# Attention's sums with the values standing still and the turned probabilities moving, and the softmax division moved to ScalarE

## The chip, the cores and the metric

The kernel runs on one core of a Trainium2 chip. Its engines are PE (TensorE, matrix multiply), DVE (VectorE), ACT (ScalarE), POOL (GpSimd) and SP (SyncE, which issues the weight loads). Each follows its own list of instructions in order, and they meet only by semaphores. The metric is the device time of one execution in microseconds (us), the median of several runs.

## The reference

A causal decoder trunk of two layers over 256 tokens of width 1024. Every layer is half a SwiGLU block, a mixer, and another half SwiGLU block, each behind an RMSNorm and added to x. The first layer's mixer has two groups of heads side by side: eight heads of softmax attention (MLA) and eight heads of a gated delta rule. Their results stand side by side (512 columns each) and go through one output projection:

```python
def one_block(args):                     # MLA attention, one block of 128 queries
    q_blk, blk = args
    sc = jnp.einsum('bhqd,bhkd->bhqk', q_blk, kh) * scale
    q_idx = blk * ATTN_BLOCK + jnp.arange(ATTN_BLOCK)
    sc = jnp.where(key_idx[None, :] <= q_idx[:, None], sc, -jnp.inf)
    p = jax.nn.softmax(sc, axis=-1)
    return jnp.einsum('bhqk,bhkd->bhqd', p, vh)
...
y = jnp.concatenate([y_mla, o.reshape(b, s, GDN_HEADS * GDN_DV)], axis=-1)
return y @ w_out
```

The softmax weights of a query are exp(score) over their sum; they then weigh the values v, 64 features per head. The delta rule needs decay matrices, triangular systems of 64x64 per head and chunk, and a scan over four chunks. Everything is float32.

## The kernel before

Matrix products of weights are made of three products of parts rounded to PE's fast float type ("hi" and "lo"): ScalarE writes the hi part of each weight unit (function hi), VectorE or POOL the lo part, and the same is done with the activations.

The change lies in the first layer's mixer, between 268 and 300 us of the execution. There the kernel runs the eight attention heads one after another, and lays the preparation of the delta rule between them. The 256 tokens are two tiles of 128, so a head has three blocks of 128x128 scores: queries 0 with keys 0, queries 1 with keys 1, queries 1 with keys 0. Per head h:

- PE makes the scores (head_scores, L1912) in one of two banks.
- VectorE finds each row's maximum (row_max, L1325 to L1327) and sends it on as the bias of the exp.
- ScalarE writes exp of the three blocks to probs (exps, L753 and L755) and gets the sum of each row beside it (row_sum). probs has two slots.
- PE turns the three blocks (transposes, L2012), ScalarE copies the result to pT (L771), and PE multiplies (weighted_values, L1927): the turned probabilities are loaded as weights, 128 columns each, and v moves, 64 columns each. The result has the tokens on the partitions and lies in banks 0 and 1.

The rows are divided by their sums at the very end: when all heads are done, VectorE takes one reciprocal of all 16 sums per token (L1405) and multiplies both banks by it on the way to Y (L1408, "y_mla"). PE then turns Y (y_transposes, L2050), ScalarE rounds it to hTh (yT_hi, L803), and VectorE writes the rest to hTl (yT_lo, L1415).

Each engine's order is written out by hand in its own block, with waits on semaphores. PE starts with head_scores of heads 0 and 1; then for each h come transposes(h), head_scores(h+2), weighted_values(h-1) and pieces of the delta rule (decay_rows, head_transposes, gram, problems). ScalarE's list has for each h the copy to pT, pieces of the delta rule (after head 0 two copies of Z, L776, and small exps, L784 to L786; after heads 1 to 4 dT_out, L761; after head 2 the exp of Dec, L791) and exps(h+2). VectorE's has row_max(h+2) and, between, norms of the delta rule's heads (L1349), the decay differences (L1377), products (L1385, L1392) and D (L1397, L1398).

Behind the heads VectorE makes ten masked blocks (L1366), the division, the first pair of N1 (L1428), two products with the decay (L1437) and yT_lo. PE takes the first two m1 products (L1981), y_transposes, and then a loop of small products for the triangular systems; its second step in that loop, dt_next(0, 1), writes to banks 0 and 1 and so waits for yT_lo. Behind that comes early (L2061), the first part of the output projection, which needs the lo parts of weights that POOL makes (L459) once the masked blocks are done. ScalarE writes two units' hi parts (L500) before yT_hi.

```python
pe.wait_ge(S("exp_done"), 2 * h + 2)                # before transposes(h)
dve.wait_ge(S("score_sums"), h + 1)                 # before row_max(h)
if n == 0:
    pe.wait_ge(S("yT_lo"), 4)                       # before dt_next(0, 1)
sp_.wait_ge(S("v_sums"), 4)                         # before the loads of the next SwiGLU's weights
```

## Time and profile before

| | |
|---|---|
| median of 3 runs | 1062.76 us (1062.66 to 1063.14) |
| the profiled execution | 1061.91 us, of which the span of the profile is 1060.0 |
| PE busy | 1046.9 us (99%), 8325 matmuls |
| VectorE (DVE) busy | 809.8 us (76%) |
| ScalarE (ACT) busy | 562.6 us (53%) |
| POOL busy | 46.7 us (4%) |
| chain that ended last | PE 80%, DVE 14%, issue 3%, ACT 2% |

The shares are means over the whole span; what the change meets is read from the stretch of the heads. The profile has six views that matter here: the page with totals; busy time by stretch; the chain of waits, which goes back from the last instruction to what released each step; the timeline of one engine, with the idle time ahead of an instruction and what ended it; one line of the program with its durations; and groups by line and shape.

### The profile page before, as it was taken

To read this page: it belongs to the slowest core of one execution; us is meant where nothing else is said; L and a number is where in the kernel's file an instruction comes from. 1 tells how busy PE (TensorE), PEld (TensorE's weight loads), DVE (VectorE), ACT (ScalarE), POOL (GpSimd) and SP (SyncE) were. 2 spreads that over 40 slices of the span, in tenths; PEclk is the share of its full clock that TensorE was granted. 3 is DMA by queue.
4 is the path that set the end of the run, shared out by engine and by line. 5 is a ranking of instruction groups with operands and counts; after the bars stand their busy time and mean duration, and the time that the engine had idled before them with its cause. 6 is when DMAs were issued, how large, how long until landed. Compare 5 with 4: busy or idle time off the path is not lost.

```text
span 1060.0 us, 19231 instructions
## 1 busy us (share of the span) xinstructions
PE 1046.9 (99%) x8325; PEld 960.7 (91%) x8325; DVE 809.8 (76%) x1072; ACT 562.6 (53%) x695; POOL 46.7 (4%) x32
## 2 busy tenths in 40 slices
PE   9999999999999999999999999999999999999998
PEld 8999987998878999998799999878888889999986
DVE  5887789899854776778987677898666548676797
ACT  6654545685873644445554444555664436444451
POOL 1000000110190000000000000001000000000000
PEclk9999999999999999999999999999999999999999
DMA  9756566463003555565556556566654546555551
GB/s 308 250 187 190 171 199 198 154 202 116 2 5 108 180 192 184 176 198 198 198 163 195 177 182 197 198 201 226 187 164 162 192 155 205 172 187 190 171 196 41
DMA packets 127214, 184.91 MB, mean 174 GB/s; under 512 B 4221, under 2 KB 101738, under 8 KB 127002
## 3 DMA queue, kind: packets, MB, share of 16 engines
q1 hardware_dynamic: 126384, 181.85, 53.1%
q0 software_dynamic: 448, 1.71, 0.5%
q8 instruction: 66, 1.08, 0.4%
q10 hardware_dynamic: 298, 0.12, 0.1%
q14 instruction: 18, 0.15, 0.0%
HBM read 182.62 MB, written 1.05 MB: 173 GB/s over the span
## 4 chain that ended last, share of the span: by engine, by line
PE 80%; DVE 14%; issue 3%; ACT 2%; DMA 1%; SPq 0%; ACTq 0%; DVEq 0%
PE banks L1528 22%; PE banks L1530 22%; PE banks L1529 22%; DVE wlo L968 3%; DVE arena L1040 2%; DVE rounded L1048 2%; PE banks L1689 1%; PE banks L1690 1%; PE banks L1691 1%; DVE arena L1041 1%; DVE raw L1042 1%; PE banks L1981 1%; DVE wlo L1050 1%; PE banks L1606 1%; PE banks L1607 1%
## 5 line engine op out<-in xcount | busy, mean ns | idle before, releaser
L960 DVE TENSOR_TENSOR wlo<-raw,whi 128x2048 fp32r<-128x2048 f32 (+2 forms) x141 | 318.7, 2271 | 101.7 <-ACT whi L500 101.7
L500 ACT ACTIVATE whi<-raw 128x2048 fp32r<-128x2048 f32 (+3 forms) x169 | 309.1, 1841 | 155.9 <-PE banks L1530 138.5
L1528 PE MATMUL banks<-xTh,whi 128*128 128x256 f32 x1360 | 385.3, 283 | 0.2 <-DVE wlo L960 0.2
L1530 PE MATMUL banks<-xTh,wlo 128*128 128x256 f32 x1360 | 384.9, 283 | 0.0
L1529 PE MATMUL banks<-xTl,whi 128*128 128x256 f32 x1360 | 384.9, 283 | 0.0
L1528 PEld LDWEIGHTS banks<-xTh,whi 128*128 128x128 f32 x1360 | 261.1, 192 | 0.4 <-DVE wlo L960 0.4
L1529 PEld LDWEIGHTS banks<-xTl,whi 128*128 128x128 f32 x1360 | 261.1, 192 | 0.0
L1530 PEld LDWEIGHTS banks<-xTh,wlo 128*128 128x128 f32 x1360 | 261.1, 192 | 0.0
L1528 PE MATMUL banks<-whi,hTh 128*128 128x512 f32 (+1 forms) x192 | 77.8, 405 | 1.6 <-DVE wlo L1050 1.6
L1530 PE MATMUL banks<-whi,hTl 128*128 128x512 f32 (+1 forms) x192 | 74.7, 389 | 0.0
L1529 PE MATMUL banks<-wlo,hTh 128*128 128x512 f32 (+1 forms) x192 | 74.5, 388 | 0.0
L562 ACT ACTIVATE rounded<-arena 128x1536 fp32r<-128x1536 f32 x24 | 35.8, 1492 | 67.4 <-DVE raw L1042 67.4
L1528 PE MATMUL banks<-whi,xTh 128*128 128x512 f32 (+1 forms) x160 | 63.2, 395 | 0.0
L556 ACT ACTIVATE rounded<-arena 128x512 fp32r<-128x512 f32 x24 | 15.2, 632 | 88.6 <-DVE arena L1024 88.6
L1530 PE MATMUL banks<-whi,xTl 128*128 128x512 f32 (+1 forms) x160 | 61.9, 387 | 0.0
L1529 PE MATMUL banks<-wlo,xTh 128*128 128x512 f32 (+1 forms) x160 | 61.8, 386 | 0.0
L1606 PE MATMUL banks<-whi,hTh 128*128 128x512 f32 x144 | 56.2, 391 | 0.0
L1607 PE MATMUL banks<-wlo,hTh 128*128 128x512 f32 x144 | 56.1, 390 | 0.0
L1528 PEld LDWEIGHTS banks<-whi,hTh 128*128 128x128 f32 x192 | 36.1, 188 | 12.2 <-DVE wlo L1050 5.0
L1610 PE MATMUL banks<-whi,hTl 128*128 128x512 f32 x144 | 44.4, 389 | 0.0
L1008 DVE TENSOR_TENSOR arena<-banks,arena 128x512 f32<-128x512 f32 x44 | 30.4, 691 | 17.9 <-PE banks L1530 17.2
L1530 PEld LDWEIGHTS banks<-whi,hTl 128*128 128x128 f32 x192 | 36.0, 188 | 7.7
(298 smaller groups left out, 1566.0 us busy)
## 6 DMA issues: line engine op xcount, KB each, us to landing
raw<-in_ffn_w_down SPq DMA_DIRECT2D x44, 1024.0 KB, 4.9
raw<-in_ffn_w_gate SPq DMA_DIRECT2D x43, 1024.0 KB, 5.3
raw<-in_ffn_w_up SPq DMA_DIRECT2D x43, 1024.0 KB, 5.4
raw<-in_sg_w_in SPq DMA_DIRECT2D x16, 1024.0 KB, 5.5
raw<-in_ab_w_in SPq DMA_DIRECT2D x8, 1024.0 KB, 5.1
raw<-in_sg_w_out SPq DMA_DIRECT2D x8, 1024.0 KB, 4.8
raw<-in_ab_w_out SPq DMA_DIRECT2D x4, 1024.0 KB, 4.9
raw<-in_ab_w_in SPq DMA_DIRECT2D x2, 832.0 KB, 4.4
```

The source lines that it names most:

```text
L500: A(whi[:, j % SLOTS, 0:n], raw[:, j % RAW_SLOTS, 0:n], ACT.Copy).then_inc(S("hi_ready"), 1)
L562: A(T_HI[k % 2], T_SUM[k % 2], ACT.Copy).then_inc(S("sums_hi"), 1)
L960: TT(wlo[:, j % RAW_SLOTS, 0:n], raw[:, j % RAW_SLOTS, 0:n], whi[:, j % SLOTS, 0:n].bitcast(f32), ALU.subtract).then_inc(S("lo_ready"), 1)
L968: TT(wlo[:, j % RAW_SLOTS, 0:1536], raw[:, j % RAW_SLOTS, 0:1536], whi[:, j % SLOTS, 0:1536].bitcast(f32), ALU.subtract)
L1008: TT(prod[:, c % 2, :], B[PAIR_BANK[c][1]][:], gate[:, c % 2, :], ALU.mult).then_inc(S("prod_ready"), 1)
L1040: link(TT(t3[:, 0:2, :], b[:, 1:3, :], bc(b[:, 3:4, :], [P, 2, 512]), ALU.add))
L1528: mm(out_ap, lh, rh, start=first, stop=False)
L1529: mm(out_ap, lh, rl, start=False, stop=False)
L1530: return mm(out_ap, ll, rh, start=False, stop=last)
L1606: mm(o, hTh[:, kk, tok], wh[:, k, c], start=kk == 0, stop=False)
L1607: mm(o, hTh[:, kk, tok], wl[:, k, c], start=False, stop=False)
L1610: last = mm(o, hTl[:, kk, tok], wh[:, k, c], start=False, stop=False)
```

## The change

The probabilities are divided by their sums before they are turned, and the second product is made the other way round.

- VectorE has a new step sum_inverse(h): it waits for both exps of head h and takes the reciprocal of its 128x2 sums. The steps for heads 0 and 1 stand ahead of the rsqrt chain, the others between the pieces for the delta rule, that for head 7 behind the first masked block. The reciprocal of all sums and the two y_mla multiplications behind the heads are gone. head_sums(1), a row sum for the delta rule, moves from behind row_max(1) to ahead of the small copies that come before row_max(0).
- ScalarE has a new step scale_probs(h): it waits for sum_inverse(h) and multiplies the head's probabilities by it in place, 128x128 and 128x256. scale_probs(0) stands behind exps(1), scale_probs(h+1) behind the copy to pT of head h.
- PE's transposes(h) wait for scale_probs(h) and no longer for the exp. In weighted_values v is now loaded as weights (64 columns) and the turned probabilities move: one product with 256 columns (both blocks of keys 0) and one with 128. The result has features on the partitions, as the output projection wants it, so Y and y_transposes(0, 4) are gone for this half; yT_hi waits for the last weighted_values.
- Two semaphores of POOL become one (dec_then_vb), with the same order.

In ScalarE's list around heads 0 to 2 there stood before (L753 and L755 are exps of heads 0, 1 and then 2, L680 a copy for the convolution, L771 the copy to pT, L776 the copies of Z):

```order
L753 ACTIVATE arena,small<-banks,small 128x128 [waits softmax_in]
L755 ACTIVATE arena,small<-banks,small 128x256
L753 ACTIVATE arena,small<-banks,small 128x128 [waits softmax_in]
L755 ACTIVATE arena,small<-banks,small 128x256
L680 ACTIVATE arena<-banks 128x2x256 [waits nt_sums]
L771 ACTIVATE arena<-banks 128x384 [waits pT_sums]
L776 ACTIVATE arena<-banks,small 128x512 [waits head_sums,unit_done]
L776 ACTIVATE arena<-banks,small 128x512
L784 ACTIVATE small<-banks 64x2x4 [waits gc_ready]
L784 ACTIVATE small<-banks 64x2x4 x3
L785 ACTIVATE small<-small 128x16
L786 ACTIVATE small<-small 128x16
```

Nothing stands there between the exps of head 1 and the copy to pT but one copy. Now the same stretch reads (L768 and L769 are scale_probs of heads 0 and 1, L779 the copy to pT, L786 the copies of Z):

```order
L753 ACTIVATE arena,small<-banks,small 128x128 [waits softmax_in]
L755 ACTIVATE arena,small<-banks,small 128x256
L753 ACTIVATE arena,small<-banks,small 128x128 [waits softmax_in]
L755 ACTIVATE arena,small<-banks,small 128x256
L768 ACTIVATE arena<-arena,small 128x128 [waits sum_inverted]
L769 ACTIVATE arena<-arena,small 128x256
L680 ACTIVATE arena<-banks 128x2x256 [waits nt_sums]
L779 ACTIVATE arena<-banks 128x384 [waits pT_sums]
L768 ACTIVATE arena<-arena,small 128x128 [waits sum_inverted]
L769 ACTIVATE arena<-arena,small 128x256
L786 ACTIVATE arena<-banks,small 128x512 [waits head_sums,unit_done]
L786 ACTIVATE arena<-banks,small 128x512
```

Two pairs of scaled copies have come in, the first ahead of the first copy to pT, the second ahead of the copies of Z, and both wait for VectorE's reciprocals.

In VectorE's list from row_max(7) to yT_lo there stood before (L1366 the masked blocks, L1405 the reciprocal, L1408 y_mla, L1428 N1, L1437 the products with the decay, L1415 yT_lo; the first row is the bias of head 7):

```order
L1327 SCALAR_TENSOR_TENSOR small<-small 128x1
L1366 TENSOR_TENSOR arena<-banks,C 128x512 [waits seed_sums] x4
L1366 TENSOR_TENSOR arena<-banks,C 128x512 [waits score_sums,seed_sums]
L1366 TENSOR_TENSOR arena<-banks,C 128x512 [waits seed_sums] x4
L1366 TENSOR_TENSOR arena<-banks,C 128x512 [waits score_sums,seed_sums]
L1405 RECIPROCAL small<-small 128x16 [waits exp_done]
L1408 TENSOR_TENSOR arena<-banks,small 128x512 [waits pv_sums,dve_chain]
L1408 TENSOR_TENSOR arena<-banks,small 128x512
L1428 TENSOR_TENSOR arena<-C,banks 128x512 [waits m1_sums] x2
L1437 TENSOR_TENSOR arena<-banks,arena 128x8x64 [waits gram_sums,dec_masked]
L1437 TENSOR_TENSOR arena<-banks,arena 128x8x64 [waits gram_sums]
L1415 TENSOR_TENSOR hTl<-banks,hTh 128x256 [waits yT_hi] x4
```

The blocks followed each other without a wait for an exp, and the division stood behind them. Now the same stretch reads (L1343 sum_inverse(7), L1383 the masked blocks, L1446 N1, L1455 the products, L1433 yT_lo):

```order
L1337 SCALAR_TENSOR_TENSOR small<-small 128x1
L1383 TENSOR_TENSOR arena<-banks,C 128x512 [waits seed_sums]
L1343 RECIPROCAL small<-small 128x2 [waits exp_done]
L1383 TENSOR_TENSOR arena<-banks,C 128x512 [waits seed_sums] x3
L1383 TENSOR_TENSOR arena<-banks,C 128x512 [waits score_sums,seed_sums]
L1383 TENSOR_TENSOR arena<-banks,C 128x512 [waits seed_sums] x4
L1383 TENSOR_TENSOR arena<-banks,C 128x512 [waits score_sums,seed_sums]
L1446 TENSOR_TENSOR arena<-C,banks 128x512 [waits m1_sums] x2
L1455 TENSOR_TENSOR arena<-banks,arena 128x8x64 [waits gram_sums,dec_then_vb]
L1455 TENSOR_TENSOR arena<-banks,arena 128x8x64 [waits gram_sums]
L1433 TENSOR_TENSOR hTl<-banks,hTh 128x256 [waits yT_hi] x4
```

Three instructions are gone between the masked blocks and N1, and a reciprocal that waits for the last exp has come in behind the first masked block.

The diff:

```diff
--- before.py
+++ after.py
@@ -452,8 +452,8 @@
             pool.wait_ge(S("decb_ready"), 1)
             pool.wait_ge(S("softmax_in"), HEADS)
             D3 = Dec.rearrange("p (m j) -> p m j", j=64)
-            mul(D3, D3, bc(const("causal").unsqueeze(1), [P, NT * HEADS, 64])).then_inc(S("dec_masked"), 1)
-            per_head(QKVn[2].rearrange("p t n -> p (t n)"), QKVn[2], beta).then_inc(S("vb_ready"), 1)
+            mul(D3, D3, bc(const("causal").unsqueeze(1), [P, NT * HEADS, 64])).then_inc(S("dec_then_vb"), 1)
+            per_head(QKVn[2].rearrange("p t n -> p (t n)"), QKVn[2], beta).then_inc(S("dec_then_vb"), 1)
             def pool_lo(j):
                 pool.wait_ge(S("hi_ready"), j + 1)
                 nc.gpsimd.tensor_tensor(wlo[:, j % RAW_SLOTS, :], raw[:, j % RAW_SLOTS, :],
@@ -761,14 +761,24 @@
                 A((kT, qT)[i // 2][:, 2 * (i % 2):2 * (i % 2) + 2, :],
                   B[3][:].rearrange("p (q n) -> p q n", n=SEQ), ACT.Copy).then_inc(S("dT_out"), 1)
 
+            def scale_probs(h):
+
+                act.wait_ge(S("sum_inverted"), h + 1)
+                p = probs[h % 2]
+                A(p[:, 0, :], p[:, 0, :], ACT.Copy, scale=rden[:, 0, h:h + 1])
+                A(p[:, 1:3, :], p[:, 1:3, :], ACT.Copy, scale=rden[:, 1, h:h + 1]).then_inc(S("probs_scaled"), 1)
+
             exps(0)
             exps(1)
+            scale_probs(0)
             nt_out(5)
             for h in range(HEADS):
                 act.wait_ge(S("pT_sums"), h + 1)
                 if h >= 2:
                     act.wait_ge(S("pv_sums"), h - 1)
                 A(pT[:, h % 2, :], B[4][:, 0:3 * P], ACT.Copy).then_inc(S("pT_out"), 1)
+                if h + 1 < HEADS:
+                    scale_probs(h + 1)
                 if h == 0:
                     act.wait_ge(S("unit_done"), Z_UNIT + 2)
                     act.wait_ge(S("head_sums"), 2)
@@ -799,7 +809,7 @@
 
             def yT_hi(k0, k1):
                 for k in range(k0, k1):
-                    act.wait_ge(S("yT_sums"), k // 2 + 1)
+                    act.wait_ge(*((S("pv_sums"), HEADS) if k < 4 else (S("yT_sums"), k // 2 - 1)))
                     A(hTh[:, k, :], B[YT_BANK[k // 2]][:, 256 * (k % 2):256 * (k % 2) + 256], ACT.Copy
                       ).then_inc(S("yT_hi"), 1)
 
@@ -1327,6 +1337,12 @@
                 STT(nbias[:, h % 2, 1:2], m[:, 1:2], m[:, 2:3], q_nscale[:, 1, h:h + 1], ALU.max, ALU.mult
                     ).then_inc(S("softmax_in"), 1)
 
+            def sum_inverse(h):
+
+                dve.wait_ge(S("exp_done"), 2 * h + 2)
+                nc.vector.reciprocal(rden[:, :, h], row_sum[:, :, h]).then_inc(S("sum_inverted"), 1)
+
+            head_sums(1)
             gcf, ekf = (a.rearrange("p t h -> p (t h)") for a in (gc, ek))
             dve.wait_ge(S("gc_sums"), 2)
             for c in range(2):
@@ -1339,7 +1355,8 @@
             dve.wait_ge(S("q_scaled"), 2)
             row_max(0)
             row_max(1)
-            head_sums(1)
+            sum_inverse(0)
+            sum_inverse(1)
             dve.wait_ge(S("head_sums"), 2)
             both = qk_head_ss.rearrange("p a m -> p (a m)")
             link(rsqrt(both, both, 2 * M, 1.0))
@@ -1370,15 +1387,19 @@
             for h in range(HEADS):
                 if 0 < h < HEADS - 2:
                     row_max(h + 2)
+                if h == 0:
+                    sum_inverse(h + 2)
                 if h == 1:
                     dve.wait_ge(S("gc_ready"), 1)
                     for t in range(NT):
                         dve.wait_ge(S("gr_sums"), t + 1)
                         link(TT(h3(Dec, t), B[(5, 2)[t]][:].rearrange("p (h j) -> p h j", j=64),
                                 bc(gcf[:, 8 * t:8 * t + 8].unsqueeze(2), [P, HEADS, 64]), ALU.subtract))
+                    sum_inverse(3)
                     TS(Dec, Dec, 0.0, None, ALU.max).then_inc(S("dec_diff"), 1)
                 if h == 2:
                     head_norm(QKVn[0], 0, float(DK) ** -0.5).then_inc(S("heads_normed"), 1)
+                    sum_inverse(4)
                     dve.wait_ge(S("decay_exps"), 2)
                     link(TT(begc, beta, egc, ALU.mult))
                     dve.wait_ge(S("decay_exps"), 3)
@@ -1391,23 +1412,20 @@
                         dst, decay = decay_products(odd, Lm, DecB)
                         TT(dst, B[(5, 2)[odd]][:].rearrange("p (q j) -> p q j", j=64), decay, ALU.mult
                            ).then_inc(S("decayed"), 1)
+                    sum_inverse(5)
                 if h == 4:
                     dve.wait_ge(S("decayed"), 2)
                     for t in range(NT):
                         link(TT(h3(D, t), h3(Lm, t), eight("first"), ALU.mult))
                         TT(h3(D, t), eight("eye64"), h3(D, t), ALU.subtract).then_inc(S("d_ready"), 1)
-
-            for n in range(5):
+                    sum_inverse(6)
+
+            masked_block(0, 0)
+            sum_inverse(7)
+            for n in range(1, 5):
                 masked_block(0, n)
             for n in range(5):
                 masked_block(1, n)
-            dve.wait_ge(S("exp_done"), 2 * HEADS)
-            link(nc.vector.reciprocal(rden, row_sum))
-            dve.wait_ge(S("pv_sums"), HEADS)
-            for t in range(NT):
-                TT(Y[:, t, 0:512].rearrange("p (h d) -> p h d", d=VDIM),
-                   B[t][:].rearrange("p (h d) -> p h d", d=VDIM),
-                   bc(rden[:, t, :].unsqueeze(2), [P, HEADS, VDIM]), ALU.mult).then_inc(S("y_mla"), 1)
 
             def yT_lo(k0, k1):
                 for k in range(k0, k1):
@@ -1430,7 +1448,7 @@
                        two_banks((M1_BANKS if n else M1_FIRST)[t]).rearrange("p o (m j) -> p o m j", j=64), ALU.subtract
                        ).then_inc(S("m1_ready"), 1)
                 if n == 0:
-                    dve.wait_ge(S("dec_masked"), 1)
+                    dve.wait_ge(S("dec_then_vb"), 1)
                     for odd in range(2):
                         dve.wait_ge(S("gram_sums"), odd + 3)
                         dst, decay = decay_products(odd, Am, Dec)
@@ -1922,10 +1940,12 @@
                 pe.wait_ge(S("pT_out"), h + 1)
                 if h == 0:
                     pe.wait_ge(S("z_out"), 2)
-                e = slice(VDIM * h, VDIM * h + VDIM)
-                for t, i, tk, a, z in ((0, 0, 0, True, True), (1, 1, 1, True, False), (1, 2, 0, False, True)):
-                    last = mm(B[t][:, e], pT[:, h % 2, P * i:P * i + P], kv_v[:, tk, h, :], start=a, stop=z)
-                last.then_inc(S("pv_sums"), 1)
+                o = B[h // 4][HC[h % 2], 256 * (h // 2 % 2):256 * (h // 2 % 2) + 256]
+                blocks3 = pT[:, h % 2, :].rearrange("p (b n) -> p b n", n=P)
+                mm(o.rearrange("p (b n) -> p b n", n=P), kv_v[:, 0, h, :], blocks3[:, 0:3:2, :], start=True, stop=False,
+                   skip_group_check=True)
+                mm(o[:, P:2 * P], kv_v[:, 1, h, :], blocks3[:, 1, :], start=False, stop=True, skip_group_check=True
+                   ).then_inc(S("pv_sums"), 1)
 
             eye = const("eye64")
 
@@ -2005,7 +2025,7 @@
             head_scores(1)
             to_tokens(5)
             for h in range(HEADS):
-                pe.wait_ge(S("exp_done"), 2 * h + 2)
+                pe.wait_ge(S("probs_scaled"), h + 1)
                 if h:
                     pe.wait_ge(S("pT_out"), h)
                 for i in range(3):
@@ -2071,8 +2091,6 @@
             m1(0, 0)
             pe.wait_ge(S("lt_level"), 10)
             m1(0, 1)
-            pe.wait_ge(S("y_mla"), 2)
-            y_transposes(0, 4)
             for n in range(4):
                 pe.wait_ge(S("m1_ready"), 2 * n + 1)
                 if n:
@@ -2128,7 +2146,7 @@
                 last.then_inc(S("qdT_sums"), 1)
             pe.wait_ge(S("at_ready"), 2)
 
-            pe.wait_ge(S("vb_ready"), 1)
+            pe.wait_ge(S("dec_then_vb"), 2)
 
             def heads(): return [(q, odd, 2 * q + odd) for q in range(PAIRS) for odd in range(2)]
 
```

## Rows read from the trace of the kernel before

**Rows 1.** The page's first line
```profile
span 1060.0 us, 19231 instructions
```

**Rows 2.** Busy time by stretch: PE, PEld, DVE, ACT, POOL, then PEclk, DMA share, GB/s
```profile
268.00:276.00 8.00, 7.03 (x51) 4.80 (x50) 7.42 (x28) 6.95 (x26) 0.00 (x0) 1.00 0.00 0
276.00:284.00 8.00, 8.00 (x127) 7.54 (x125) 7.80 (x18) 6.81 (x19) 0.00 (x0) 1.00 0.01 2
284.00:292.00 8.00, 7.62 (x167) 7.06 (x165) 7.01 (x14) 4.59 (x14) 3.32 (x2) 1.00 0.01 3
292.00:300.00 8.00, 6.54 (x279) 5.78 (x281) 7.93 (x17) 7.04 (x11) 6.29 (x3) 1.00 0.02 5
```

**Rows 3.** The chain of waits in order of time: start us, us, what
```profile
288.32 0.21 DVE small L1327
...
289.06 3.77 DVE arena L1366 x7
...
295.92 1.27 DVE arena L1428 x2
...
298.33 1.40 DVE hTl L1415 x4
...
299.86 0.41 PE banks L1981 x11
...
300.96 0.43 PE banks L1528
```

**Rows 4.** Timeline of PE: start us, us, what [idle before <-releaser]
```profile
269.65 0.55 PE L2012 MATMUL banks<-C,arena 128*128 128x128 f32 x3 [0.84 <-ACT arena L755]
...
277.00 0.78 PE L1927 MATMUL banks<-arena 128*128 128x64 f32 x6
...
294.57 0.69 PE L1981 MATMUL banks<-arena 64*64 64x64 f32 x32 [0.21 <-DVE arena L1366]
```

**Rows 5.** Timeline of ScalarE (ACT), the same columns
```profile
270.38 0.20 ACT L755 ACTIVATION_READ_ACCUMULATOR arena<-banks,small 128x1 f32 x1
...
270.47 0.60 ACT L680 ACTIVATE arena<-banks 128x512 f32<-128x512 f32 x1
...
270.94 0.50 ACT L771 ACTIVATE arena<-banks 128x384 f32<-128x384 f32 x1
...
271.31 1.29 ACT L776 ACTIVATE arena<-banks,small 128x512 f32<-128x512 f32 x2
...
274.13 0.46 ACT L753 ACTIVATE arena<-banks,small 128x128 f32<-128x128 f32 x1 [0.57 <-DVE small L1327]
...
275.03 0.20 ACT L755 ACTIVATION_READ_ACCUMULATOR arena<-banks,small 128x1 f32 x1
...
292.56 3.71 ACT L500 ACTIVATE whi<-raw 128x2048 fp32r<-128x2048 f32 x2
```

**Rows 6.** Timeline of VectorE (DVE), the same columns
```profile
270.45 0.18 DVE L937 TENSOR_SCALAR small<-small 128x32 f32<-128x32 f32 x1
...
275.15 0.55 DVE L1325 TENSOR_REDUCE small<-banks 128x3 f32<-128x384 f32 x1
...
278.78 1.22 DVE L1349 SCALAR_TENSOR_TENSOR arena<-arena,small 128x1024 f32<-128x1024 f32 x1
...
287.66 0.56 DVE L1325 TENSOR_REDUCE small<-banks 128x3 f32<-128x384 f32 x1 [0.88 <-PE banks L1912]
...
294.44 0.24 DVE L1405 RECIPROCAL small<-small 128x16 f32<-128x16 f32 x1
```

**Rows 7.** Line 671 alone: durations ns min/median/max, first and last start
```profile
L671 ACT ACTIVATE arena<-arena,param_cols x12: 493/496/510, 214.9 to 251.7; 128x256 f32<-128x256 f32 x12
```

**Rows 8.** Groups by line and form, 262 to 300: busy us, mean ns
```profile
L1927 PE MATMUL banks<-arena 128*128 128x64 f32 x48 | 6.3, 268 | 0.0
...
L1935 PE MATMUL banks<-arena,C 64*64 64x512 f32 x8 | 2.2, 611 | 0.1
```

**Rows 9.** Timeline of POOL (GpSimd)
```profile
294.62 9.07 POOL L459 TENSOR_TENSOR wlo<-raw,whi 128x2048 fp32r<-128x2048 f32 x2 [1.71 <-DVE arena L1366]
```

## The prediction

> **What bounds the kernel now.** I read the page's first line, then the busy time by stretch, then the chain of waits, then each engine's timeline around the attention heads. The profiled execution took 1061.91 us, 1060.0 of it the span [rows 1], 0.85 less than the median 1062.76 of the three runs; the change below is worked out inside that span and then added to the median. It acts between 268 and 300 us. There [rows 2] the granted clock is 1.00, and of each 8 us PE is busy 7.03, 8.00, 7.62 and 6.54, VectorE 7.42, 7.80, 7.01 and 7.93, ScalarE 6.95, 6.81, 4.59 and 7.04. So PE and VectorE run neck and neck through the heads, ScalarE has 5.7 us free in the first three stretches, and after 292 VectorE leads. The chain [rows 3] agrees: behind the heads it runs through VectorE's masked blocks, the first pair of N1 at 295.92, the products with the decay and the four yT_lo from 298.33, and comes back to PE at 299.86, at the first step that needs yT_lo. From there PE leads. The weight loads of the next part wait for v_sums, which lies behind this, so nothing keeps its old time and a shift at 299.86 goes through to the end.
>
> **What goes.** From the start of the reciprocal, 294.44, to that of N1, 295.92 [rows 3, 6], VectorE's path loses 1.48 us: the reciprocal and both y_mla. PE's eight transposes of y_mla go too; I count them at nothing, since PE waits for VectorE's decay products and yT_lo right behind them. The yT_hi on ScalarE lose their wait for PE, but stand behind two weight copies (hi), 292.56 to 296.27 [rows 5].
>
> **What comes on ScalarE and VectorE.** A scaled copy of 128x256 within SBUF takes 0.50 us [rows 7]. ScalarE's slope is 0.9 ns per column (1.85 for one of 2048 columns against 0.37 from 270.94 to 271.31 for 384 [rows 5]), so one of 128x128 takes 0.39. An instruction lets the next start 0.13 before its own end (270.94 plus 0.50 against 271.31). So scale_probs holds ScalarE for 0.65 us per head and its result stands 0.77 after its start; eight make 5.2 us. A reciprocal of 128x16 takes 0.24 [rows 6]; one of 128x2 isn't in the trace. Between nothing and 0.24 I take 0.1 of queue.
>
> **What comes on PE.** The old sums are six instructions of 64 moving columns: 0.78 us, less the last one's own 0.27, is 0.51 from first to last start, 0.10 each [rows 4, 8]. The new ones are two passes of 256 columns and two of 128. 448 more columns cost 0.61 - 0.27 = 0.34 [rows 8], so 768 columns take 0.59 where the six took 0.61. If the four loads of 64 columns came on top, at half of 0.10, it would be 0.2 more per head. Bounds: nothing and 0.2; I take 0.1, most of which falls into PE's new waits.
> The Trainium skill ("TensorE: Matmul & The Clock Gate", Part 3, The mechanism) says that a weight load overlaps running matmuls only where the row group differs. All loads here use all 128 rows, so by it the 0.2 would be due and the sum below would be 2.0 instead of 1.8. The trace can't decide: 0.10 fits a covered load as well as half of one followed by 64 columns.
>
> **What comes on the path.** Now transposes(h) wait for scale_probs(h), that for sum_inverse(h) on VectorE, and that for the last exp of h. Behind a waiting inverse stand the next row_max and all of VectorE's decay work.
> *Heads 0 and 1.* head_sums(1) moves ahead into idle time, but the inverse of head 1 waits for the second exp, whose sum is out at 270.58 [rows 5]. With the wake-up and both reciprocals the rsqrt chain starts near 270.8, not 270.45 [rows 6]: 0.35 later.
> *Head 2.* ScalarE takes its next instruction at 270.47, so the first scaled probabilities stand at 271.24 and transposes(0) start near 271.3, not 269.65 [rows 4]. They take 0.55, pT 0.37, scale_probs(1) 0.65; so the two Z copies start at 272.9, not 271.31. The small exps behind them ended at 273.56 (274.13 less the idle 0.57) and end now at 275.15; exp(2), 1.10 long (274.13 to 275.23), has its sums at 276.25 [rows 5]. VectorE, which was free for row_max(3) at 275.15 [rows 6], comes to the inverse at 275.5, waits 0.8, and row_max(3) starts at 276.4: 1.25 later.
> *Head 4.* ScalarE's queue from 276.15: pT 0.37, scale 0.65, dT_out 0.47 (a 512-wide copy, 270.47 to 270.94), exps 1.0, pT 0.37, scale 0.65, to 279.66; dT_out again with about 0.25 of waiting for PE, the exp of Dec (1024 columns, 0.93 by the slope), exps 1.10: sums out at 282.4 [rows 5]. VectorE left head_norm at 279.92 (278.78 plus 1.22 less overlap [rows 6]), now about 281.5, waits 0.9, and goes on at 282.6: 2.7 later. Head 3's own short wait is contained in that.
> *Heads 5 and 6.* Two reciprocals and a little wait: 2.95 later. But before row_max(7) VectorE idled 0.88, until 287.66, for the scores of head 7 [rows 6]. Now it is the late one: 286.78 plus 2.95, so 289.75, 2.1 later. PE's scores come about then too, since its problems wait for VectorE.
> *Head 7.* From row_max(7) to its bias is 0.87 (288.32 plus 0.21), exp(7) follows with 1.10, so its sum is out 2.0 after row_max(7). Its inverse stands behind the first masked block, which lets go 1.40 after (289.06 [rows 3]). It waits 0.66 and takes 0.1: the masked blocks end 2.86 later.
> *Behind them.* 1.48 less. And the second N1 now meets its matmuls: m1(0,1) begins 0.05 after the last block and takes 0.69 [rows 4], so N1 starts 0.26 later than VectorE could; y_mla covered that.
> Sum at 299.86: 2.1 + 0.76 - 1.48 + 0.26 = 1.64, and with 0.15 for PE's sums **1.8 us later**. Two covers hold: the weight copies start 2.9 later, so the first yT_hi pair is out at 299.7, and VectorE wants it at 300.1; POOL's first split ends at 294.62 + 4.55 + 2.9 = 302.05 [rows 9], and PE wants it at 300.96 + 1.8 = 302.75 [rows 3]. Ends of the unknown: reciprocals, copies and wake-ups each 0.1 cheaper give 1.2; each 0.1 dearer, with PE's 0.2, give 3.0.
>
> **The rivals.**
> *ScalarE becomes the bound* (slower). 18.35 us busy of the first 24, plus 5.2, leaves 0.5 [rows 2]; each head passes its ordered queue three times, and yT_hi has only 0.4 of cover. At the dear end it is 3.0 us and somewhat more, 1065.8 to 1066.5; it decides once a pair of scaled copies holds ScalarE over 0.75. Against it: PE and VectorE have work of their own for most of those waits. VectorE did this scaling in some 1.25 us over 1024 columns, ScalarE gets 3072; were all its 5.2 us on the path, it would be 5.2 - 1.48 = 3.7, so 1066.5.
> The Trainium skill ("ScalarE: Activation LUTs", Rules for kernel authors) gives multiplications to VectorE rather than ScalarE; by that rule this rival would be the likeliest, while the rows show free time on ScalarE for most of the copies.
> *The heads take the lag in* (faster). If ScalarE catches up before exp(2) and exp(4), the waits of 0.8 and 0.9 vanish, the idle 0.88 before row_max(7) takes in the rest, and -1.48 + 0.26 are left: 1061.5. It needs ScalarE to have 1.6 us to spare before exp(2), where it had 0.57 [rows 5].
> *TensorE's clock falls* (slower). PE would idle 0.84 + 1.65 = 2.5 us before transposes(0), where 0.84 were [rows 4]; the granted clock was 1.00 throughout [rows 2]. On the lower of the two levels PE's next four us of work take four more, one to two of which lie in its waits: 2 to 3 on top, 1066.6 to 1067.6.
>
> **How the numbers follow.** The forecast, 1062.76 + 1.8 = 1064.6, has 0.55, ScalarE as the bound 0.28, the clock 0.07, the heads that take it in 0.10. A measurement of this kernel can tell about 0.2%, 2.1 us, from no change; the forecast lies just inside it. Of its 0.55 I put 0.46 inside and 0.09 above; of ScalarE's 0.28, 0.05 inside; all of the clock's above; of the faster case 0.02 inside. That gives slower 0.39, within 0.53, faster 0.08. The forecast's own range is 1063.9 to 1065.8 (1.2 to 3.0 added); for 8 in 10 I take 1062.5 to 1066.8.
>
> **What would show it.** Right: transposes(0) near 271.3; VectorE waiting about 0.8, 0.9 and 0.7 before the inverses of heads 2, 4 and 7; row_max(7) 2.1 and the end of the masked blocks 2.9 later; no wait before yT_lo; the first step behind yT_lo 1.8 later, and the same shift from there to the end. Wrong: row_max(7) unmoved, matmuls at twice their duration behind transposes(0), yT_lo waiting for ScalarE, or a shift that changes after 301.

## The result: slower by 0.5%, outside the range, and the profile after

The changed kernel takes 1068.16 us (median of 6 runs, 1067.25 to 1068.99), the kernel before in the same session 1062.80 (1062.66 to 1063.26, 6 runs): a ratio of 1.005, 95% interval [1.0037, 1.0063]. It is 5.36 us slower; the forecast said 1.8.

The profiled execution of the changed kernel has this first line, beside [rows 1]:

```profile
span 1065.4 us, 19204 instructions
```

Its granted clock is the first thing that differs. These are busy times by stretch, the columns those of [rows 2]: first the 8 us of the first row there, then the same time in pieces of 2 us.

```profile
268.00:276.00 8.00, 5.49 (x29) 3.60 (x27) 5.88 (x25) 7.50 (x26) 0.00 (x0) 0.79 0.00 0
...
270.00:272.00 2.00, 0.59 (x4) 0.59 (x5) 1.12 (x8) 1.85 (x7) 0.00 (x0) 0.90 0.00 0
272.00:274.00 2.00, 2.00 (x11) 1.65 (x12) 1.33 (x8) 1.79 (x5) 0.00 (x0) 0.50 0.00 0
274.00:276.00 2.00, 2.00 (x9) 0.70 (x8) 1.95 (x4) 1.87 (x9) 0.00 (x0) 0.74 0.00 0
276.00:278.00 2.00, 2.00 (x14) 1.29 (x13) 1.26 (x5) 1.72 (x7) 0.00 (x0) 1.00 0.00 0
```

It was 1.00 all through before. Now it is 0.50, the lower of its two levels (1.2 GHz), from about 271.6 to about 275. PE's timeline (start us, us, what [idle before <-releaser]) shows what PE did before and behind:

```profile
268.30 0.60 PE L1839 MATMUL banks<-C,arena 128*128 128x128 f32 x4
271.41 0.76 PE L2032 MATMUL banks<-C,arena 128*128 128x128 f32 x3 [2.51 <-ACT arena L769]
...
273.80 1.66 PE L1955 MATMUL banks<-arena,C 64*64 64x512 f32 x4
275.39 0.55 PE L2032 MATMUL banks<-C,arena 128*128 128x128 f32 x3
```

PE stood still for 2.51 us, waiting for the second scaled copy (L769). Then transposes(0) took 0.76 instead of 0.55 [rows 4], and transposes(1) start at 275.39. In the kernel before they stood at 272.22, behind four products of 512 columns that took 1.07 and now take 1.66:

```profile
271.21 1.07 PE L1935 MATMUL banks<-arena,C 64*64 64x512 f32 x4
272.22 0.55 PE L2012 MATMUL banks<-C,arena 128*128 128x128 f32 x3
```

VectorE's timeline has the waits at the inverses of heads 2, 3, 4 and 7 (L1343), the last row_max (L1335), the masked blocks (L1383) and N1 (L1446):

```profile
276.68 0.17 DVE L1343 RECIPROCAL small<-small 128x2 f32<-128x2 f32 x1 [0.70 <-ACT arena L755]
...
280.94 0.17 DVE L1343 RECIPROCAL small<-small 128x2 f32<-128x2 f32 x1 [1.50 <-ACT arena L755]
...
284.42 0.17 DVE L1343 RECIPROCAL small<-small 128x2 f32<-128x2 f32 x1 [0.80 <-ACT arena L755]
...
292.08 0.56 DVE L1335 TENSOR_REDUCE small<-banks 128x3 f32<-128x384 f32 x1 [0.52 <-PE banks L1930]
...
294.12 0.17 DVE L1343 RECIPROCAL small<-small 128x2 f32<-128x2 f32 x1 [0.56 <-ACT arena L755]
294.21 5.45 DVE L1383 TENSOR_TENSOR arena<-banks,C 128x512 f32<-128x512 f32 x9
299.66 1.51 DVE L1446 TENSOR_TENSOR arena<-C,banks 128x512 f32<-128x512 f32 x2
```

The last row_max stood at 287.66 [rows 6] and N1 at 295.92 [rows 3]: 4.4 and 3.7 later. Then the second surprise, on PE, between the first of the eight early products (L1546 here, L1528 before, where the first stood at 300.96 in the chain [rows 3]) and the fifth:

```profile
304.47 0.50 PE L1546 MATMUL banks<-whi,hTh 128*128 128x512 f32 x1
...
306.06 1.63 PE L2001 MATMUL banks<-arena 64*64 64x64 f32 x96 [0.62 <-issue]
...
309.88 1.29 PE L2001 MATMUL banks<-arena 64*64 64x64 f32 x68 [0.69 <-issue]
...
313.52 0.81 PE L2001 MATMUL banks<-arena 64*64 64x64 f32 x41 [0.50 <-issue]
...
317.14 0.45 PE L2001 MATMUL banks<-arena 64*64 64x64 f32 x12 [0.48 <-issue]
```

Four waits "issue", 2.3 us in all, that no engine ends. In the kernel before there were two in the same stretch, 0.75 in all:

```profile
310.58 0.80 PE L1981 MATMUL banks<-arena 64*64 64x64 f32 x36 [0.20 <-issue]
...
314.26 0.34 PE L1981 MATMUL banks<-arena 64*64 64x64 f32 x8 [0.55 <-issue]
```

In the changed kernel they come 3.6 to 3.8 us apart. From one to the next PE runs 126 to 128 recorded matmuls, each with its weight load. The DMA view of the same kernel from 302 to 322 us (GB/s in slices of 0.5 us; then the queue, its packets, MB) shows what comes at that pace:

```profile
GB/s 0 0 0 33 0 0 0 0 0 0 33 0 0 0 0 0 0 0 33 0 0 0 0 0 0 33 0 0 0 0 0 0 33 0 0 0 0 0 0 0
...
q8 instruction: 5, 0.08, 1.7%
```

A packet of instructions arrives at 303.5, 307, 311, 314.5 and 318, 33 GB/s times 0.5 us or 16.5 KB each, and PE goes on 2.5 to 3 us behind each. The Trainium skill ("Perfetto Trace Analysis", The 4-stage abstract model) says that an instruction has 64 bytes; by that, as an estimate, a packet holds about 256, and the 126 to 128 matmuls with as many loads agree.

To compare kernels whose earlier work drifts by some tenths, I count from the start of the last product of the Z unit ahead of the heads (262.62 before, 262.71 after). Shifts against the kernel before, in us:

| kernel | ratio | transposes(0) | row_max(7) | N1 | first early | eighth early |
|---|---|---|---|---|---|---|
| changed | 1.005 | 1.67 | 4.33 | 3.65 | 3.49 | 5.11 |
| e1 fill, same place | 1.0029 | 1.67 | 2.72 | 2.03 | 3.23 | 4.54 |
| e2 fill, other place | 1.0020 | 1.67 | 2.72 | 2.03 | 2.07 | 3.63 |
| e3 no division | 1.0003 | 0 | 0.84 | -0.40 | -0.57 | 0.47 |
| e4 copies alone | 1.0039 | 1.67 | 5.71 | 5.02 | 4.86 | 7.33 |
| e5 inverses alone | 1.001 | 0 | 0.97 | 0.20 | 0.12 | 2.03 |
| e6 copies, clock held | 1.0017 | 1.66 | 2.67 | 1.98 | 1.82 | 2.84 |
| e7 longer gap alone | 1.004 | 2.51 | 3.67 | 3.68 | 3.46 | 3.94 |
| e8 removal alone | 0.9997 | 0 | 0 | -1.48 | -0.85 | 0.47 |
| e9 gap as after | 1.0028 | 1.71 | 2.82 | 2.82 | 2.61 | 3.46 |
| e10 gap, clock held | 1.0008 | 1.71 | 1.25 | 1.25 | 0.85 | 2.87 |
| e11 before, wide | 0.9969 | 0 | 0 | 0 | -0.27 | -2.39 |
| e12 removal, wide | 0.9969 | 0 | 0 | -1.48 | -0.58 | -2.69 |
| e13 before, all wide | 0.996 | 0 | 0 | 0 | -0.43 | -2.57 |
| e14 removal, all wide | 0.995 | 0 | 0 | -1.48 | -1.59 | -3.74 |
| e15 change, all wide | 0.9982 | 1.67 | 2.71 | 2.02 | 1.86 | -0.29 |

The ratio is over all executions, but the shifts of each row are from one profiled execution. That of the kernel before took 1061.91 us, 1.0 to 1.6 less than its medians in the sessions of the experiments (1062.87 to 1063.49). Up to N1 this does not show. The last column, which contains the "issue" waits, can be too large by about that much: e2 has 3.63 there, and its median is 1.6 above that of the kernel before.

### The profile page after: what moved, and what is told of

It reads as the page before. It is cut to its first block, busy times and chain, and to the rows that moved or that the text cites. A ratio compares the mean times of both kernels' runs of the same rounds, so it can differ in the third digit from the quotient of the medians.

```text
span 1065.4 us, 19204 instructions
## 1 busy us (share of the span) xinstructions
PE 1050.0 (99%) x8301; PEld 959.9 (90%) x8301; DVE 809.4 (76%) x1077; ACT 568.2 (53%) x711; POOL 46.8 (4%) x32
## 3 DMA queue, kind: packets, MB, share of 16 engines
q0 software_dynamic: 448, 1.71, 0.5%
## 4 chain that ended last, share of the span: by engine, by line
PE 80%; DVE 14%; issue 3%; ACT 2%; DMA 1%; SPq 0%; ACTq 0%; DVEq 0%
PE banks L1546 22%; PE banks L1548 21%; PE banks L1547 21%; DVE wlo L978 3%; DVE arena L1050 2%; DVE rounded L1058 2%; PE banks L1707 1%; PE banks L2001 1%; PE banks L1709 1%; PE banks L1708 1%; DVE arena L1051 1%; DVE raw L1052 1%; DVE wlo L1060 1%; PE banks L1624 1%; PE banks L1628 1%
## 5 line engine op out<-in xcount | busy, mean ns | idle before, releaser
L1546 PE MATMUL banks<-xTh,whi 128*128 128x256 f32 x1360 | 385.4, 283 | 0.2 <-DVE wlo L970 0.2
L1546 PEld LDWEIGHTS banks<-xTh,whi 128*128 128x128 f32 x1360 | 261.2, 192 | 0.4 <-DVE wlo L970 0.4
L1546 PE MATMUL banks<-whi,hTh 128*128 128x512 f32 (+1 forms) x192 | 77.7, 405 | 1.5 <-DVE wlo L1060 1.3
L1546 PE MATMUL banks<-whi,xTh 128*128 128x512 f32 (+1 forms) x160 | 63.2, 395 | 0.0
L1546 PEld LDWEIGHTS banks<-whi,hTh 128*128 128x128 f32 x192 | 36.1, 188 | 12.1 <-DVE wlo L1060 4.9
```

Of the source, the lines that this page charges most:

```text
L1546: mm(out_ap, lh, rh, start=first, stop=False)
```

## The experiments

Theory: three things add up, the forecast's mechanism (about 2 us), the fall of the clock (about 1.6) and PE's supply of instructions, which takes back what the removal gains (about 1.2). Rivals: the round trip over VectorE costs it all; ScalarE's queue does, whatever the clock.

### The clock

Both fills keep PE at work in the gap and change nothing else of the changed kernel, e1 by the first loop, e2 by the second:

```diff
             to_tokens(5)
+            for _ in range(12):
+                mm(B[4][:, 3 * P:3 * P + 64], ident, ident[:, 0:64], start=True, stop=True)
...
+            for _ in range(36):
+                mm(B[4][:, 3 * P:4 * P], mask16[:, 0:P], mask16[:, P:2 * P], start=True, stop=True)
```

> The changed kernel with twelve float32 products of 64 columns (24 instructions, results unused) on PE between to_tokens(5) and transposes(0), where PE idled 2.51 us. They also bring PE's list behind y_mla's old place back to the instruction count of the kernel before. Theory 1, the clock: the granted clock stays 1.00 from 270 to 276 us, transposes(0) take 0.55 and not 0.76 us, row_max(7) comes about 2.1 us after that of the kernel before and not 4.4, and the time falls by about 2.3 to 1065.9. Theory 2, PE's waits of 0.5 to 0.7 us without a cause in the trace between 305 and 317 us hang on where PE's list of instructions is cut: with the old count they shrink from 2.3 to about 0.75 us and the time falls by another 1.5, to 1064.4. Rival, the queue on ScalarE bounds whatever PE's clock does: 1068 as the changed kernel.

> As before, but the gap is filled with 36 bfloat16 products of 128 columns, so the clock should hold as well while PE's list behind is 12 instructions pairs longer than in the kernel before. Theory 1: clock 1.00, row_max(7) plus 2.1, about 1065.9 if the unexplained waits stay at 2.3. Theory 2: the waits without a cause move to other places; their sum may come out anywhere between 0.7 and 2.3, so 1064.4 to 1065.9. Rival (ScalarE bounds): 1068.

e1 took 1066.17 us, ratio 1.0029 [1.0018, 1.0040], e2 1065.04, ratio 1.0020 [1.0010, 1.0029]. The second theory of e1 fell: with the old count of instructions the "issue" waits from the first to the eighth early product are still 2.1 us, and two more, 1.7 in all, stand ahead of the first. e2 by stretch and on PE's timeline:

```profile
272.00:274.00 2.00, 2.00 (x15) 1.21 (x13) 1.69 (x10) 1.85 (x5) 0.00 (x0) 1.00 0.00 0
...
269.11 2.17 PE L2028 MATMUL banks<-mask 128*128 128x128 bf16 x36
271.79 0.55 PE L2034 MATMUL banks<-C,arena 128*128 128x128 f32 x3 [0.51 <-ACT arena L769]
```

The clock stays at 1.00, the transposes start at the same place (8.70 us behind the Z unit) and take 0.55, and N1 comes 1.62 us earlier than in the changed kernel. The rival "ScalarE, whatever the clock" falls: only 2.03 of the 3.65 at N1 is left.

The gap alone, put into the kernel before by GpSimd (three products in e7, two in e9, and in e10 two with the 36 products of e2):

```diff
+            pool.wait_ge(S("exp_done"), 2)
+            for _ in range(2):
+                after(mul(at(11008, 256), QKVn[2][:, 0, 0:256], QKVn[2][:, 1, 0:256]))
...
                 pe.wait_ge(S("exp_done"), 2 * h + 2)
+                if h == 0:
+                    pe.wait_ge(S("pool_chain"), 10)
```

> The kernel before, but its first transposes wait for three products of 256 columns on GpSimd behind the exps of head 0, so that PE stands idle some 2.5 us there instead of 0.84; nothing else is changed. Theory (the idle time alone makes the granted clock fall): a stretch of some 4 us from the transposes on below 0.8, transposes(0) 0.7 to 0.8 long instead of 0.55, N1 2 to 4 us later, ratio 1.002 to 1.004. Rival (the clock fell for another reason, or the idle time is harmless): clock 1.00, N1 at most 1.2 us later, ratio 1.000 to 1.0012.

> The kernel before with GpSimd's two products (instead of three) ahead of the first transposes: they should start 8.7 to 8.8 us behind the Z unit's last product, as in the changed kernel; nothing else is changed. Theory (this idle time alone makes the granted clock fall): a stretch of about 4 us from 270 on below 0.8, N1 2.4 to 3.4 us later than in the kernel before, ratio 1.002 to 1.004. Rival (only the longer idle time of the run before did): clock 1.00, N1 at most 1.7 later, ratio at most 1.0015.

> As e9_gap_as_after, with 36 small products on PE in the idle time. Theory (the clock is the larger part of what the idle time costs): clock 1.00, N1 0.5 to 1.5 us later than in the kernel before and at least 1 us earlier than in e9_gap_as_after, ratio 1.0002 to 1.0015. Rival (the late start of the transposes is what costs, whatever the clock): N1 within 0.5 of that of e9_gap_as_after, ratio 1.002 to 1.003.

e7: 1067.67 us, ratio 1.0040 [1.0027, 1.0053]; its gap was 3.35 us, longer than meant, hence e9. Its transposes(0) took 0.52 and not the 0.7 to 0.8 expected; the clock fell just behind them. e9: 1066.31, ratio 1.0028 [1.0018, 1.0038]. e10: 1064.01, ratio 1.0008 [0.9999, 1.0017]. e9 on PE's timeline and by stretch:

```profile
271.88 0.52 PE L2017 MATMUL banks<-C,arena 128*128 128x128 f32 x3 [2.55 <-POOL arena L424]
...
272.00:274.00 2.00, 2.00 (x13) 1.61 (x14) 1.69 (x10) 1.57 (x4) 0.00 (x0) 0.69 0.00 0
274.00:276.00 2.00, 2.00 (x7) 0.52 (x4) 1.93 (x5) 1.88 (x11) 0.00 (x0) 0.50 0.00 0
```

Without any part of the change, the same idle time makes the clock fall; with it held (e10, 1.00 from 268 to 300) N1 comes 1.57 earlier, and the median is 2.3 lower. So 1.6 us at N1 is the clock's price, found twice.

The fall does not come in every execution. Where it came, the mean clock of the whole execution is 0.996 to 0.998. It is 1.00 in one of the eight of e9 (1063.43 us, the others 1065.04 to 1067.24) and in one of the six of e4 below (1065.00, the others 1067.02 to 1070.16). It is 0.998 in one of the nine of e2 (1067.59, the others 1064.50 to 1066.46) and in one of the six of e1 (1068.26, the others 1065.05 to 1066.95). These four differ from the median of the others of their kernel by 2.5 to 3.3 us. They were not profiled, so where their clock fell or held is not shown.

### Which part of the change costs the rest

e3 takes out all steps of the division, e5 only ScalarE's, so in both the transposes wait for the exps. The edit of e3:

```diff
-            scale_probs(0)
...
-                if h + 1 < HEADS:
-                    scale_probs(h + 1)
...
-                nc.vector.reciprocal(rden[:, :, h], row_sum[:, :, h]).then_inc(S("sum_inverted"), 1)
...
-                pe.wait_ge(S("probs_scaled"), h + 1)
+                pe.wait_ge(S("exp_done"), 2 * h + 2)
```

e4 takes out the reciprocal and keeps the copies, which multiply by one:

```diff
-                act.wait_ge(S("sum_inverted"), h + 1)
...
-                A(p[:, 0, :], p[:, 0, :], ACT.Copy, scale=rden[:, 0, h:h + 1])
...
+                act.wait_ge(S("exp_done"), 2 * h + 2)
+                A(p[:, 0, :], p[:, 0, :], ACT.Copy, scale=ones128[:, 0:1])
...
```

e6 is e4 with the 36 products of e2.

> The changed kernel without the division: no sum_inverse, no scale_probs, and transposes(h) wait for the exps as before (the probabilities stay unscaled). What is left is the second product the other way round, without y_mla and PE's y_transposes. My sum says 1.48 less on VectorE, 0.26 back at the second N1 and 0 to 0.15 for PE: 1061.6 to 1061.8, with the clock at 1.00 since transposes(0) start near 269.7. Rival, the new product with 768 columns is what costs: 1063 or more.

> The changed kernel without VectorE's inverses: scale_probs multiplies by a constant of one, waits for ScalarE's own exp and for nobody else. Transposes(0) come about as late as in the changed kernel (271.4), so by theory 1 the clock falls here too, and with it most of the loss stays: 1065.5 to 1067. Rival, the round trip over VectorE (its waits of 0.7, 1.5, 0.8 and 0.56 us before the inverses) is the cause: 1062.5 to 1063.5.

> VectorE makes the eight small inverses where the change puts them, but ScalarE scales nothing and the transposes wait for the exps as before, so the division is left out. Theory (the scaled copies and the idle PE ahead of the first transposes cost the time, the inverses hardly any): transposes(0) 7.0 us behind the last product of the Z unit as in the kernel before, granted clock 1.00, first pair of N1 between 0.4 earlier and 0.5 later than before, ratio 0.999 to 1.001. Rival (VectorE standing at its inverses is what costs): N1 1.5 us or more later, ratio 1.0015 to 1.003.

> Scaled copies by one without inverses (the division is left out), and 36 small products on PE ahead of the first transposes, which keep it from standing idle. Theory (most of what the copies alone lost was the granted clock): clock 1.00 through the heads, first pair of N1 1.5 to 2.2 us later than in the kernel before instead of 5.0, ratio 1.001 to 1.0025. Rival (the copies hold ScalarE's queue, whatever the clock): N1 over 3 us later, ratio 1.003 to 1.005.

e3: 1063.53 us, ratio 1.0003 [0.9994, 1.0011]. e4: 1067.93, ratio 1.0039 [1.0026, 1.0052]. e5: 1063.48, ratio 1.001 [0.9999, 1.002]. e6: 1064.93, ratio 1.0017 [1.0009, 1.0026].

e3 missed: its time lies where the rival had it, and not at 1061.6 to 1061.8. Up to the scores of head 7 PE's list differs from that of before in the new products alone, and PE gets to these scores 0.84 later. So row_max(7) is 0.84 later too, and VectorE waits 1.22 us for it instead of 0.88 [rows 6]:

```profile
289.51 0.56 DVE L1332 TENSOR_REDUCE small<-banks 128x3 f32<-128x384 f32 x1 [1.22 <-PE banks L1926]
```

So without any division the new products take back more than half of the 1.48. e4 came out 0.9 above its range. The rival "round trip over VectorE" falls with e4, which has no inverses and loses as much, its clock being low for longer:

```profile
272.00:274.00 2.00, 2.00 (x11) 1.82 (x9) 0.21 (x2) 1.50 (x5) 0.00 (x0) 0.50 0.00 0
274.00:276.00 2.00, 2.00 (x6) 0.29 (x4) 1.63 (x4) 1.88 (x9) 0.00 (x0) 0.50 0.00 0
276.00:278.00 2.00, 2.00 (x12) 1.80 (x10) 0.35 (x1) 1.99 (x7) 0.00 (x0) 0.50 0.00 0
```

With the clock held the copies alone (e6) put N1 1.98 later, as much as copies and inverses together (e2, 2.03). The inverses alone (e5) cost 0.20 there against 0.40 gained with neither (e3): 0.6. So the copies are most of what the change costs at N1 with the clock held: 2.4 us more than with neither. How much of the new products' 0.84 is hidden behind the waits for them is not shown. And even without any division (e3) the changed form does not win.

### What takes the gain back

e8 is the kernel before without the reciprocal and y_mla; PE turns what stands in Y:

```diff
-            link(nc.vector.reciprocal(rden, row_sum))
...
-                TT(Y[:, t, 0:512].rearrange("p (h d) -> p h d", d=VDIM),
...
-            pe.wait_ge(S("y_mla"), 2)
```

e11 is the kernel before with half as many instructions in the later steps of the triangular systems (w is 2 there), e12 is e8 with the same. e13 and e14 are these two with the first step wide too, all but m1(0, t), and e15 is e2 in that form:

```diff
-                for i in range(HEADS // 2):
+                for i in range(0, HEADS // 2, w):
...
-                            right = eye[HC[r], :] if rhs is None else rhs[t][HC[r], rhs_at(h):rhs_at(h) + 64]
-                            last = mm(banks[HC[r ^ s], pair[s], 64 * i:64 * i + 64], left, right,
+                            at0 = 0 if rhs is None else min(rhs_at(h), 512 - 64 * w)
+                            right = eye[HC[r], :] if rhs is None else rhs[t][HC[r], at0:at0 + 64 * w]
+                            last = mm(banks[HC[r ^ s], pair[s], 64 * i:64 * i + 64 * w], left, right,
```

> The kernel before without VectorE's reciprocal and its two scaled copies into Y behind the masked blocks; PE transposes what stands in Y, so the attention's result is left out; the heads are untouched. Theory (what is gained there is given back, since PE then waits for its own instructions, 16 KB every 3.4 to 3.9 us): first pair of N1 1.0 to 1.4 us earlier, first product with yT_lo about 1 us earlier, eighth such product at most 0.5 earlier, ratio 0.9993 to 1.000. Rival (the forecast's way of adding: the gain at N1 goes through to the end): eighth product and end 1.2 to 1.5 earlier, ratio 0.9985 to 0.999.

> The kernel before, with half as many instructions in the small products of the later steps of the blocks' inverses: two products of 64 columns become one of 128, with the weights of the first, so that the values are not the attention's. Theory (PE waits there for its own instructions): the waits without a releaser between the first and the eighth product with yT_lo vanish (under 0.3 us in all), the instruction packets come 5 us apart and more, that stretch is 17 us long or shorter instead of 17.85. Rival (those waits have nothing to do with the number of instructions): 0.5 us or more of such waits remain.

> As e11_before_wide, and without the reciprocal and the two scaled copies as in e8_removal_alone (the attention's result is left out). Theory (the supply of instructions took the gain of e8_removal_alone back): with half the instructions the gain goes through, the eighth product with yT_lo 0.9 to 1.5 us earlier than in e11_before_wide, the median 0.8 to 1.5 us below that of e11_before_wide. Rival (the gain is lost at another engine, GpSimd's splits or ScalarE's copies): the eighth product less than 0.5 earlier, the median within 0.5 us.

> As e11_before_wide, with the first step of the blocks' inverses in products of 128 columns too (all but the first two m1); the values are not the attention's. It is the base of the next two. Theory: no waits without a releaser from N1 to the eighth product with yT_lo, that product as in e11_before_wide or up to 0.6 us earlier.

> e13_before_all_wide without the reciprocal and the two scaled copies (the attention's result is left out). Theory (the supply of instructions took the gain back): first product with yT_lo 0.9 to 1.4 us and the eighth 0.8 to 1.4 us earlier than in e13_before_all_wide, median 0.7 to 1.5 us lower. Rival (another engine takes it back): the eighth product less than 0.5 us earlier, the median within 0.5 us.

> The changed kernel with the 36 small products that hold the clock and with the products of 128 columns of e13_before_all_wide (the values are not the attention's). Theory (what the forecast added up is right and passes through once neither the clock falls nor the instructions run short): N1 1.8 to 2.3 us, first and eighth product with yT_lo 1.5 to 2.3 us later than in e13_before_all_wide, median 1.3 to 2.4 us above it. Rival (the change costs more behind N1 by another way, ScalarE's yT_hi or GpSimd's split): the eighth product 3 us or more later, median 2.8 us or more above.

e8: 1062.54 us, ratio 0.9997 [0.9988, 1.0006]. N1 is 1.48 earlier, exactly what went; the first early product 0.85, the eighth 0.47 later. Its PE timeline:

```profile
299.85 0.57 PE L1974 MATMUL banks<-arena 64*64 64x64 f32 x21 [0.44 <-issue]
...
307.43 1.16 PE L1974 MATMUL banks<-arena 64*64 64x64 f32 x64 [0.57 <-issue]
...
311.04 0.80 PE L1974 MATMUL banks<-arena 64*64 64x64 f32 x36 [0.47 <-issue]
...
315.26 0.34 PE L1974 MATMUL banks<-arena 64*64 64x64 f32 x8 [1.09 <-issue]
```

PE reaches its work sooner and waits for its instructions instead, 2.6 us where the kernel before had 0.75. The median is 0.3 us lower, with an interval from 1.3 lower to 0.6 higher, so the times alone do not tell whether the gain is lost. e11: 1059.37 us, ratio 0.9969 [0.9956, 0.9981], no "issue" wait from N1 to the eighth early product, and from the first to the eighth 15.7 us instead of 17.85. The DMA view of e11 from 302 to 322:

```profile
GB/s 0 0 0 0 0 0 33 0 0 0 0 0 0 0 0 0 0 0 0 0 33 0 0 0 0 0 0 0 0 33 0 0 0 0 0 0 0 0 33 0
```

The packets are now 4.5 to 7 us apart. The stretch has seven steps from one early product to the next. The two that held a wait in the kernel before give 1.45 of the 2.1 us, the other five 0.67, some of it because the wide products of a step are shorter themselves (1.54 us against 1.63). So the supply held the kernel before up there too, by some 1.2 us (an estimate: 1.45 less 0.1 for each of the two steps). e12 missed: 1059.19 us, ratio 0.9969 [0.9957, 0.998], counted from transposes(0) its eighth early product is only 0.29 earlier than in e11 and not 0.9. Its trace has the reason, a wait ahead of the first early product, in the step that was left narrow:

```profile
301.88 0.57 PE L1975 MATMUL banks<-arena 64*64 64x64 f32 x21 [0.71 <-issue]
```

With that step wide as well: e13 1059.01 us, ratio 0.9960 [0.9947, 0.9972]; e14 1058.00, ratio 0.9950 [0.9936, 0.9963]; e15 1061.17, ratio 0.9982 [0.9973, 0.9991]. None has an "issue" wait from N1 to the eighth early product. First and eighth early product of e13, e14 and e15 (Z unit's last product at 263.30, 262.60 and 263.19):

```profile
301.14 0.50 PE L1528 MATMUL banks<-whi,hTh 128*128 128x512 f32 x1
...
316.85 0.50 PE L1528 MATMUL banks<-whi,hTh 128*128 128x512 f32 x1
```

```profile
299.28 0.50 PE L1521 MATMUL banks<-whi,hTh 128*128 128x512 f32 x1
...
314.98 0.50 PE L1521 MATMUL banks<-whi,hTh 128*128 128x512 f32 x1
```

```profile
303.32 0.50 PE L1546 MATMUL banks<-whi,hTh 128*128 128x512 f32 x1
...
319.02 0.51 PE L1546 MATMUL banks<-whi,hTh 128*128 128x512 f32 x1
```

All three take 15.7 us from the first to the eighth, so now a shift does pass unchanged. The removal gains 1.16 at the first, 1.17 at the eighth and 1.01 in the median (e14 against e13). And the change, with the clock held and instructions enough, costs 2.02 at N1, 2.29 at the first, 2.28 at the eighth and 2.16 in the median (e15 against e13): the forecast's term by itself.

So of the 5.36 us some 2.2 are the mechanism that was forecast. The clock costs 1.6 at N1 and more at the end: 2.3 by the medians of e9 and e10, 2.5 to 3.3 between executions of one kernel, and some 3.2 by the ratios of the changed kernel and e2. Why it grows behind N1 is not shown. These two, 4.5 to 5.5 together, already fill the 5.36. That the supply also takes back the removal's gain of 1.0 to 1.2 is seen in the traces of e8 and e14, but the medians do not settle it: e2, whose instructions run short too, is 1.1 to 3.1 us behind the kernel before, and the mechanism alone makes 2.2.

No kernel here gives the same result faster than the kernel before: the wide ones compute something else, and e2, the best form of the change, stays 0.2% behind it. A form of the triangular systems with the right values and fewer instructions was not tried.

## Why the prediction was wrong

**The clock had 0.07, and nothing in the sum.** This is the step that failed. The idle time ahead of transposes(0) was forecast right (2.5 us, 2.51 measured), but the sum took the products behind it at their old durations. The clock fell to 0.50, four products took 1.66 instead of 1.07, and N1 came 1.6 later for it. With the clock held (e2) the change costs 1.6 us by the medians and 2.1 by the ratio, around the 1.8 of the forecast. The evidence against the fall was a clock of 1.00 behind an idle time of 0.84, which says nothing about 2.5. The rival's price of 2 to 3 us is near the 2.3 to 3.3 found at the end, in part by luck: its four us of work at the lower level stand in no row, and in the trace PE had done less than half of that when the clock rose again near 275.

**"the same shift from there to the end"** failed as well. The shift is 3.5 us at the first early product and 5.1 at the eighth. The chain of waits had said "From there PE leads", which is true, but part of PE's time was waiting for instructions; in the trace of before two small "issue" waits showed it, and I passed over them. How much of the 1.6 comes from the change and how much from the one execution that was profiled stays open.

**What goes.** 1.48 us at N1 is exact (e8), and 1.2 of it reaches the first early product where instructions are not short (e14), as -1.48 + 0.26 said. In the trace of e8 nothing of it reaches the eighth early product; the median of e8 leaves that open.

**ScalarE and VectorE.** Scaled copies of 0.40 and 0.51, the reciprocal 0.17, transposes(0) at 271.41 against 271.3, the rsqrt chain at 270.79 against 270.8:

```profile
270.56 0.40 ACT L768 ACTIVATE arena<-arena,small 128x128 f32<-128x128 f32 x1
270.85 0.51 ACT L769 ACTIVATE arena<-arena,small 128x256 f32<-128x256 f32 x1
...
270.79 0.16 DVE L947 TENSOR_SCALAR small<-small 128x32 f32<-128x32 f32 x1
```

**The waits.** 0.70, 0.80 and 0.56 where 0.8, 0.9 and 0.66 were forecast; head 3's short wait became 1.50 behind the low clock. With the clock held (e15) the four are 0.90, 0.59, 0.95 and 0.56, and row_max(3), (5) and (7) are 1.30, 3.02 and 2.71 later, where the sum had 1.25, 2.7 and 2.1. The last was 0.6 too small, because "Now it is the late one" was wrong: VectorE came 3.2 later (2.95 forecast) and still waited for the scores of head 7, as e15 shows:

```profile
290.94 0.56 DVE L1335 TENSOR_REDUCE small<-banks 128x3 f32<-128x384 f32 x1 [0.36 <-PE banks L1930]
```

With it the sum was too small, 1.8 against 2.2.

**PE's sums.** One head in the changed kernel:

```profile
295.69 0.65 PE L1945 MATMUL banks<-arena 128*64 128x256 f32 x2
296.17 0.38 PE L1947 MATMUL banks<-arena 128*64 128x128 f32 x2
296.49 0.69 PE L2001 MATMUL banks<-C,arena 64*64 64x64 f32 x32
```

From their start to the next work is 0.80; the old six took 0.61 to 0.73 (the last head, 0.85 in both kernels, is left aside). That is 0.1 to 0.2 more, so the Trainium skill's rule on weight loads ("TensorE: Matmul & The Clock Gate", Part 3, The mechanism), by which 0.2 were due, fits as well as my 0.1. In e3 the new products came to 0.84 at row_max(7), where the sum had 0.15 in all.

**The covers.** GpSimd's first split was used up to the last tenth: it began when ScalarE had written hi, 5.1 us later than before (3.5 with the clock held, e15) where the sum had 2.9, and ended, 4.55 later, at 304.4, just as the first early product began.

```profile
299.85 9.09 POOL L459 TENSOR_TENSOR wlo<-raw,whi 128x2048 fp32r<-128x2048 f32 x2 [2.52 <-ACT whi L500]
```

**The other rivals.** ScalarE as the bound whatever the clock fell with e2, though its copies are most of what e2 keeps at N1 (e6). That the heads take the lag in was wrong in every run with the copies: row_max(7) is 2.67 later or more.

## What to carry to other kernels

Before you add a shift up, look at what bounds the stretch behind it: where an engine waits at even distances for nothing that the trace names, look at its instruction packets. Here such waits took a gain back in one trace (e8), and they differ from one execution to the next, so that a single profile of each kernel does not price them. Where a change makes PE stand still for longer than the trace of before ever shows, the old granted clock is no evidence; a few cheap products in the gap tell, and here they brought the ratio from 1.005 to 1.002. Price each removal by a kernel that makes it alone.

## What the hardware showed

- PE's instruction packets, 16.5 KB, come 3.5 to 4 us apart where PE runs small products without a pause. The waits this makes, 0.2 to 1.1 us each, differ from profile to profile; with half as many instructions (e11, e13) they are gone. What sets the time of a packet stays open.
- The clock fell behind 2.51, 2.55 and 3.35 us of idle PE in this place and stayed at 1.00 behind 0.84, and behind a gap that was filled with 36 products of 128 columns (e2, e6, e10, e15). All this is from the profiled executions; one of the eight of e9 has a mean clock of 1.00.
